# Counted filler matmuls on TensorE in the first stage of a one-core transformer step

## The reference

```python
def rmsnorm(x, g):
    xf = x.astype(jnp.float32)
    y = xf * lax.rsqrt(jnp.mean(xf * xf, axis=-1, keepdims=True) + EPS)
    return (y * g.astype(jnp.float32)).astype(x.dtype)

z = rmsnorm(x, norm_mix) @ w_in        # (320, 2048) @ (2048, 4160)
c_q, c_kv, k_r, gate_b, gate_c, h = jnp.split(z, IN_SPLITS, axis=-1)
...
# latent attention and a gated convolution on z, w_o, residual,
# then a router and 32 experts (top 2), residual, final rmsnorm
```

## Time and profile before

| | |
|---|---|
| median of 3 runs | 1521.53 us |
| lowest, highest | 1520.55, 1521.89 us |
| the profiled execution's own time | 1520.34 us |
| its span in the trace | 1518.4 us |
| TensorE matmul busy | 1343.2 us, 88% of the span |
| VectorE, ScalarE busy | 590.5 us, 347.6 us |
| HBM traffic | 312 GB/s mean over the span |

### The profile page before, as it was taken

How to read it: one execution, slowest core, us unless ns; L and a number is a source line. 1 busy time by engine, 2 the same in 40 slices (tenths; PEclk the granted TensorE clock), 3 DMA queues, 4 the chain that set the end, 5 groups by cost and what they waited for, 6 DMA issues and landing times.

```text
span 1518.4 us, 22122 instructions
## 1 busy us (share of the span) xinstructions
PE 1343.2 (88%) x8510; PEld 714.2 (47%) x8511; DVE 590.5 (39%) x1175; ACT 347.6 (23%) x595; POOL 32.4 (2%) x41
## 2 busy tenths in 40 slices
PE   6999999999999999787888888888889988888885
PEld 4989999566666663232222222322323322232221
DVE  4335444044574443242243234224324422332344
ACT  5332322123453322111111111111212111111113
POOL 1000000000000000000000000000000000000000
PEclk9999999999999989999898888988989989898887
DMA  9454451023353368999999999999989999999994
GB/s 324 131 166 137 161 167 61 10 70 111 92 180 112 131 285 355 408 432 430 432 433 432 429 433 433 431 429 433 433 369 400 432 434 432 428 434 432 432 428 180
DMA packets 69751, 473.91 MB, mean 312 GB/s; under 512 B 9532, under 2 KB 46656, under 8 KB 55824
## 3 DMA queue, kind: packets, MB, share of 16 engines
q1 hardware_dynamic: 68640, 470.78, 76.0%
q0 software_dynamic: 832, 2.48, 0.4%
q10 hardware_dynamic: 240, 0.09, 0.0%
HBM read 469.97 MB, written 3.38 MB: 312 GB/s over the span
## 4 chain that ended last, share of the span: by engine, by line
PE 52%; DMA 41%; DVE 3%; issue 2%; ACT 1%; DVEq 0%; SPq 0%; ACTq 0%
DMA ring<-in_w_down 41%; PE ps L888 11%; PE ps L587 5%; PE ps L588 5%; PE ps L589 5%; PE ps L873 3%; PE ps L649 2%; PE ps L676 2%; PE ps L739 2%; PE ps L740 2%; PE ps L741 2%; PE ps L752 2%; PE ps L850 2%; PE ps L670 1%; PE ps L879 1%
## 5 line engine op out<-in xcount | busy, mean ns | idle before, releaser
L1566 DVE TENSOR_TENSOR hreg<-ps,hreg 128x512 f32<-128x512 f32 (+1 forms) x396 | 239.4, 677 | 291.6 <-PE ps L899 291.6
L873 PE MATMUL ps<-ring,mix 128*32 128x512 f32 x2112 | 278.4, 675 | 31.7 <-DMA ring<-in_w_up 19.5
L888 PE MATMUL ps<-ring,mix 128*32 128x512 f32 x1056 | 165.7, 784 | 62.5 <-DMA ring<-in_w_down 54.7
L899 PE MATMUL ps<-mix 32*128 32x512 f32 (+1 forms) x792 | 156.3, 612 | 26.4 <-ACT mix L1249 25.6
L1206 ACT COPY mix<-ps 128x512 f32<-128x512 f32 x66 | 70.5, 1068 | 446.4 <-PE ps L873 446.4
L873 PEld LDWEIGHTS ps<-ring,mix 128*32 128x32 f32 x2112 | 74.5, 121 | 206.3 <-issue 176.2
L587 PE MATMUL ps<-xT_hi,w_hi 128*128 128x320 f32 (+1 forms) x528 | 165.6, 314 | 2.9 <-DVE w_lo L1301 2.9
L588 PE MATMUL ps<-xT_lo,w_hi 128*128 128x320 f32 (+1 forms) x528 | 164.6, 312 | 0.0
L589 PE MATMUL ps<-xT_hi,w_lo 128*128 128x320 f32 (+1 forms) x528 | 164.5, 312 | 0.0
L1301 DVE TENSOR_TENSOR w_lo<-ring,w_hi 128x1024 fp32r<-128x1024 f32 (+1 forms) x66 | 76.8, 1204 | 110.5 <-ACT w_hi L1019 110.5
L888 PEld LDWEIGHTS ps<-ring,mix 128*32 128x32 f32 x1056 | 39.6, 138 | 162.7 <-issue 104.4
(11 more groups left out here) (258 smaller groups left out, 1186.5 us busy)
## 6 DMA issues: line engine op xcount, KB each, us to landing
ring<-in_w_gate SPq DMA_DIRECT2D x31, 4096.0 KB, 22.2
ring<-in_w_up SPq DMA_DIRECT2D x31, 4096.0 KB, 23.7
ring<-in_w_down SPq DMA_DIRECT2D x31, 4096.0 KB, 23.7
ring<-in_w_in SPq DMA_DIRECT2D x32, 1024.0 KB, 8.2
ring<-in_w_o SPq DMA_DIRECT2D x16, 1024.0 KB, 6.7
ring<-in_w_up SPq DMA_DIRECT2D x2, 2048.0 KB, 11.7
ring<-in_w_gate SPq DMA_DIRECT2D x2, 2048.0 KB, 8.4
ring<-in_w_down SPq DMA_DIRECT2D x2, 2048.0 KB, 22.3
```

The lines of the kernel that those rows point to most:

```text
L873: last = pe.matmul(ps[r:r + B, bank, :], x[:, k % 4, k // 4, :], w[:, k, :], start=k < 4, stop=k >= KC - 4)
L888: last = pe.matmul(ps[B * j:B * (j + 1), 4, :], h[:, c, :], w[:, c, 512 * j:512 * j + 512], start=c == 0, stop=c == 3)
L899: pe.matmul(ps[0:tn, COMB_BANKS[u % 8], :], gates[r, t0:t0 + tn], rows[r, :], start=True, stop=True).then_inc(full_sem, 1)
L1566: dve.tensor_tensor(h, ps[0:tn, COMB_BANKS[u % 8], :], h, ALU.add).then_inc(signal, 1)
```

## The change

A function `warm(count)` issues `count` matmuls of `ones` by `ones`, 128x128 by 128x128 in float32, into bank 6, whose content nobody reads then. They wait for nothing and signal nothing. 28 of them stand ahead of the parameter rows' transpose, 10 between tile 0 and tile 1 of the first six chunks, 7 ahead of the wait for tile 2, and one ahead of `claim` in each of chunks 6 to 15: 55 in all, so 110 matmul records. TensorE also waits once for `s_ones`. Nothing is removed or reordered.

```diff
+            def warm(count):
+                for _ in range(count):
+                    pe.matmul(ps[:, SSQ_BANK, 0:P], ones[:, :], ones[:, :], start=True, stop=True)
+
+            pe.wait_ge(s_ones, 1)
+            warm(28)
             pe.wait_ge(s_ident, 16)
             pe.wait_ge(s_par, 16 * 5)
             pe.wait_ge(s_par_pool, 16 * 3)
...
             for i in range(2):
+                if i:
+                    warm(10)
                 pe.wait_ge(x_scaled, i + 1)
                 for c in range(RB):
                     if i == 0:
                         claim(pe, f"xt{c}")
                     token_tile_T(c, i)
+            warm(7)
             pe.wait_ge(x_scaled, 3)
             for c in range(KC):
                 if c >= RB:
+                    warm(1)
                     claim(pe, f"xt{c}")
                     token_tile_T(c, 0)
                     token_tile_T(c, 1)
```

## The result

| | median, us | runs | ratio to before |
|---|---|---|---|
| before | 1520.63 | 12 | |
| after | 1528.84 | 12 | 1.0053, 95% interval [1.0043, 1.0064] |

The change makes the kernel slower by half a per cent, 8.2 us. The profiled execution was the fastest of the twelve: 1524.65 us, span 1522.5, 4.1 over the span before. So the two traces can show where 4.1 us went, not the whole 8.2.

The account below looks back on a forecast made before the run. TensorE was taken to bound the kernel up to about 560 us, then streaming expert weights. First-stage terms 0 + 4.7 - 0.1 - 1.4 + 0.1 - 1.8 = +1.5 us on 1521.53 gave 1523.0, range 1520.3 to 1529.0.

Parts of the forecast that it names:

- The 28: Fillers ahead of the parameter rows' transpose: cost 0, at most a few tenths of a us, and no gain by itself.
- The gap: TensorE's idle wait for ScalarE's copy of `par`: the clock is lost there, and TensorE starts at 1.2 GHz at 14.59.
- Tile 2: Its first transpose, behind the 10 and 7 fillers: near 21.0 us instead of 16.27, 4.7 us later (3.8 to 7.1).
- Chunk 0 to chunk 6: Stretch from chunk 0 complete to chunk 6's start, 1.68 us before, set by two conversions: -0.1 us.
- Loop: Transposes of chunks 6 to 15, 9.15 us before: 7.75 at 2.4 GHz, -1.4 us, with +0.1 for waiting on VectorE.
- First projection: Its matmuls start near 30.4 us instead of 27.1, at 0.147 apart from the start: -1.8 us if at 2.4 GHz.
- Sum at the end of the stage: All first-stage terms, 0 + 4.7 - 0.1 - 1.4 + 0.1 - 1.8: +1.5 us.
- The carrying over: From the first stage to the kernel's end: a microsecond there is a microsecond at the end, in either direction.
- Rival B: Chunk loop: transposes with one filler a chunk do not keep the clock; +6.5 us, 1528.0; chance 0.15.
- Rival C: First stage: the fillers of ones do not lift the clock at all; +10.9 us, 1532.4; chance 0.07.
- Rival A: Wait for the copy of `par`: the clock holds across it; -0.5 us, 1521.0; chance 0.07.
- Rival D: After the first stage: the delay is swallowed in later waits or the experts' stream; 0 us, 1521.5; chance 0.05.

Follow-up runs that it names:

- e7: Changed kernel without its 28 head fillers, 16 short ones there for length, `keep_clock` split, 256 instructions longer than before: 1522.37 us, 1.0011 to before.
- e3: Changed kernel with all 55 fillers and three `keep_clock` matmuls split in four, 256 instructions longer than before: 1523.08 us, 1.0012 to before.
- e5: Kernel before plus 28 head fillers, 15 ahead of chunk 5's claim, 2 ahead of chunk 6's, one a chunk after; 256 instructions longer: 1516.99 us, 0.9975.
- e9: e5 with `keep_clock` left unsplit, 220 instructions longer than before, the length of the changed kernel: 1522.58 us, 1.0018 to before.
- e2: Kernel before plus the 28 head fillers, six short ones and all seven `keep_clock` matmuls split, 220 instructions longer: 1528.74 us, 1.0046 to before.
- e4: Kernel before plus 28 head fillers and 15 in the wait ahead of chunk 5's claim, `keep_clock` split, 256 instructions longer: 1519.59 us, 0.9987.
- e6: e5 without the single fillers, 3 instead of 2 ahead of chunk 6's claim, six `keep_clock` matmuls split, 256 longer than before: 1519.80 us, 0.9996 to before.
- e8: Changed kernel without the single fillers of chunks 6 to 15, 256 instructions longer than before: 1524.14 us, 1.0023 to before.
- e12: Kernel before plus only 12 `keep_clock` matmuls between the skip and expert 0's down matmuls, 48 instructions longer: 1530.24 us, 1.0057 to before.
- e1: Changed kernel with only the 28 head fillers, the 10, the 7 and the single ones removed, 112 instructions longer than before: 1523.61 us, 1.0016 to before.

## Why the prediction was right and where it was wrong

Right, with measured beside forecast, is the first stage: a filler is 0.216 us at 2.4 GHz (20 records in 4.03, part of them at the low rate; the 14 in 1.73 are 0.11 apart). The 28 cost nothing (`par` at 10.11, before 10.02) and bought nothing (e7). The gap lost the clock (0.51 after 14.6). Tile 2: 21.0 forecast, 20.77. Chunk 0 to chunk 6: 1.6 and 1.59. Loop: 7.75 forecast, 8.13, a chunk 0.84 instead of 0.8. First projection: 30.4 forecast, 30.49, and at the high rate. Sum at the end of the stage: +1.5 forecast, 30.49 - 27.10 - 1.8 = +1.6, +1.5 at 109 us, and 1.8 (0.2 to 3.3) by the ratio of e3, where the changed kernel has the short wait of before at the skip.

Wrong was the likeliest time, 1523.0, and with it the forecast of no measurable change. The step that failed is the sum itself: it priced each filler's time and had no term for its length as code, and so took the stage's +1.5 us for the whole change at the end. The carrying over ("A microsecond in the first stage is thus a microsecond at the end") is not what failed: at 256 more, +2.1 us in the first stage (31.0 - 27.1 - 1.8) gave +1.8 at the end (e3), and -3.8 gave -3.8 (e5). What was missing: at 220 instructions more the skip in expert 0 costs 5.8 us instead of 1.0, expert 1's `w_down` is requested 3.9 us later (596.92 against 593.04), and the saturated stream ends later, 4.1 us in these two traces. From 220 to 256 the medians fall by 5.8 us (after and e3; 6.2 by the ratios) and by 5.6 (e9 and e5; 6.5 by the ratios). 1.8 and some 6 make the 8.2. This sum is no cleaner than its intervals: e2 has nothing on the path and loses 7.0 (5.0 to 9.0) all the same, and of the 6 us only the later request's 3.9 are seen in a trace.

Rival B gave 1528.0, and the measured time is near it and inside the forecast's range (up to 1529.0, which B had set) by accident: its mechanism (the clock falls in the loop with one filler a chunk) did not happen in the changed kernel. It does happen without the fillers (e4, e6, e8). The rule of the page "TensorE: Matmul & The Clock Gate" of the Trainium skill, Part 4, that transposes do not engage the full rate, agrees with the 9 us of the earlier trace rows and with these three runs, but each of the three also had a wait for VectorE of about 1 us ahead of the fall, so whether transposes count for nothing or for less stays open. Rival C fell with the first row: 56 filler records at 0.213 would take 12 us, they took 8.11. Rival A's condition, the clock held across the gap, was made in e4 and e5: the gap can be bridged, if the fillers stand in it. Rival D fell in e3 and e5, whose change in the first stage is still there at the end, and in e12.

That the wait is for a code transfer is shown: it ends 1.5 to 1.7 us after one has landed in all the traces, short or long, and the length alone moves it (e2, e3, e9). That the transfer holds the skip's target is argued; no run shows the block itself, nor what the transfer waits for in the 3 to 4 us before it begins. Why 192 costs more than 220, and why e1's wait lies among the down matmuls, was not taken apart.

## What to carry to other kernels

Put a filler inside the wait that it is to fill: behind the wait it is work on the path, and the same fillers moved a few lines up turn a loss of 1.8 us (e3) into a gain of 3.8 (e5). An instruction also has a length. If a kernel has a jump while its DMA engines are saturated (busy nearly all the time), look for an "issue" wait of several microseconds behind the jump before and after each edit, and compare two versions at a length that is equal modulo 256 instructions, or the edit's own effect can be buried: here 0, 48, 256 and 304 more had the short wait, 112, 192 and 220 a long one. And where the transfers are the bound, ask of each delay which request it holds back: a `w_down` requested 9.5 us late was 9.0 us at the end.

## What was not expected of the hardware

A few dozen instructions in a corner of the program moved a 1520 us kernel by 5.8 us with no change in the result or the array time (after and e3), and making it longer made it faster. And the sum of such waits says little: in the first turn of the experts' loop the kernel before stands another 6.46 us, and so do the others (5.2 to 6.8 us), again until 1.3 to 1.7 us after a code transfer has landed, while e1 has no such wait there and only its 3.62 us at expert 0. In all it waits half as long as before, and is not faster for it: its two requests for `w_down` come 3.1 us later (596.14 instead of 593.04) and then 3.7 us earlier (620.28 instead of 623.98), and the spans are equal. That the time won at the second is not on the path of a load is my reading; no run tests it.
